# FFN gate/up products by Strassen's scheme: seven block products in place of eight, their mixed operands made on GpSimd, VectorE and ScalarE

## The reference, cut to what matters

```python
def rms_norm(x, g):
    y = xf * lax.rsqrt(jnp.mean(xf * xf, axis=-1, keepdims=True) + RMS_EPS)
    return (y * g.astype(jnp.float32)).astype(x.dtype)

def swiglu(u, wg, wu, wd):
    return (jax.nn.silu(u @ wg) * (u @ wu)) @ wd

for l in range(DEPTH):                      # DEPTH = 2
    hp = hp + 0.5 * swiglu(rms_norm(hp, norm_ffn1[l]), ffn1_wg[l], ffn1_wu[l], ffn1_wd[l])
    ...
    hp = hp + 0.5 * swiglu(rms_norm(hp, norm_ffn2[l]), ffn2_wg[l], ffn2_wu[l], ffn2_wd[l])
```

## Time and profile before

| what | value |
|---|---|
| median of 3 runs | 2280.02 us (2279.99 to 2283.45) |
| the profiled execution's span | 2286.5 us, 6.5 us over that median |
| TensorE busy | 2122.0 us, 93% of the span |
| VectorE, ScalarE, GpSimd busy | 57%, 28%, 10% |
| mean granted TensorE clock | 0.952 of 2.4 GHz |

### The profile page before, as it was taken

The page is one execution under the profiler, slowest core; times in us unless marked ns, Lnnn a source line. Parts: engine busy times, 40 slices in busy tenths (PEclk is TensorE's granted clock), DMA queues, the critical chain, the costliest instruction groups (busy, mean ns, idle before and its releaser), DMA issues.

```text
span 2286.5 us, 36127 instructions
## 1 busy us (share of the span) xinstructions
PE 2122.0 (93%) x14822; PEld 1614.0 (71%) x14822; DVE 1296.4 (57%) x1866; ACT 631.6 (28%) x630; POOL 230.5 (10%) x215
## 2 busy tenths in 40 slices
PE   6999989999997779899997999999899689999799
PEld 4777757665776746677775777777667467777577
DVE  7555566314987553555554646555655675555562
ACT  4222242112153241222224213222512032222410
POOL 1000020000047300000003000000110300000200
PEclk9999999997999789899998999999999789999899
DMA  3222212210221010022221212222222102222130
GB/s 146 92 84 82 104 58 96 82 47 10 65 65 42 15 74 19 28 83 92 92 93 63 102 55 74 89 76 92 87 85 73 53 21 92 92 91 87 70 108 37
DMA packets 23980, 166.46 MB, mean 73 GB/s; under 512 B 3024, under 2 KB 3024, under 8 KB 8176
## 3 DMA queue, kind: packets, MB, share of 16 engines
q1 hardware_dynamic: 22176, 157.98, 19.6%
q0 software_dynamic: 1744, 7.66, 1.0%
HBM read 161.80 MB, written 3.83 MB: 72 GB/s over the span
## 4 chain that ended last, share of the span: by engine, by line
PE 80%; DVE 9%; issue 5%; POOL 3%; ACT 2%; DMA 0%; ACTq 0%; DVEq 0%; SPq 0%; POOLq 0%
PE ps L1287 65%; PE ps L1281 6%; POOL arena L323 3%; DVE arena L1042 2%; DVE smalls L1041 2%; PE ps L1394 2%; PE ps L1473 1%; PE ps L1413 1%; PE ps L1589 1%; PE ps L1275 1%; PE ps L1549 0%; ACT wslot L485 0%; ACT arena L486 0%; DVE arena L1217 0%; PE ps L1377 0%
## 5 line engine op out<-in xcount | busy, mean ns | idle before, releaser
L1287 PE MATMUL ps<-normed,arena 128*128 128x296 f16 x8448 | 1073.0, 290 | 10.8 <-ACT normed L501 10.8
L1287 PEld LDWEIGHTS ps<-normed,arena 128*128 128x128 f16 x8448 | 830.1, 98 | 253.3 <-issue 11.5
L1287 PE MATMUL ps<-arena 128*128 128x296 f16 x4224 | 550.9, 295 | 50.4 <-POOL arena L323 45.5
L1287 PEld LDWEIGHTS ps<-arena 128*128 128x128 f16 x4224 | 418.4, 100 | 182.9 <-POOL arena L323 48.0
L486 ACT ACTIVATE arena<-wslot,scales 128x2048 f16<-128x2048 f32 (+1 forms) x112 | 238.7, 2131 | 366.2 <-PE ps L1287 238.9
L805 DVE TENSOR_REDUCE scales<-wslot 128x1 f32<-128x2048 f32 (+1 forms) x120 | 299.1, 2493 | 8.8 <-DMA wslot<-in_w_dn 8.7
L828 DVE SCALAR_TENSOR_TENSOR arena<-wslot,scales,arena 128x2048 f16<-128x2048 f32 (+1 forms) x112 | 282.0, 2518 | 33.2 <-ACT arena L486 32.1
L844 DVE SCALAR_TENSOR_TENSOR arena<-ps,scales,act_out 128x592 f32 (+1 forms) x88 | 73.3, 833 | 354.1 <-ACT act_out L494 353.8
L317 POOL PARTITION_ALL_REDUCE scales<-scales x120 | 49.7, 414 | 1597.2 <-DVE scales L805 1562.3
L1281 PE MATMUL ps<-normed,wslot 128*128 128x296 f32 x640 | 167.3, 423 | 1.5 <-DVE normed L773 1.0
L494 ACT ACTIVATE act_out<-ps,scales 128x592 f32<-128x592 f32 x88 | 66.2, 752 | 362.9 <-PE ps L1287 362.4
(11 more groups left out here) (250 smaller groups left out, 1301.7 us busy)
## 6 DMA issues: line engine op xcount, KB each, us to landing
wslot<-in_w_up SPq DMA_DIRECT2D x88, 1024.0 KB, 4.8
wslot<-in_w_dn SPq DMA_DIRECT2D x32, 1408.0 KB, 6.0
wslot<-in_w_in SPq DMA_DIRECT2D x20, 512.0 KB, 3.5
arena<-in_w_out SPq DMA_DIRECT2D x1, 4096.0 KB, 12.2
resid<-in_x SPq DMA_DIRECT2D x4, 592.0 KB, 6.6
out_y<-resid SPq DMA_DIRECT2D x8, 296.0 KB, 4.5
arena<-in_w_ai POOLq DMA_DIRECT2D x1, 2048.0 KB, 10.3
arena<-in_w_pool POOLq DMA_DIRECT2D x1, 1024.0 KB, 5.5
```

The lines of the kernel that those rows point to most:

```text
L1287: last = mm(ps[:, bank + hf, 0:HALF], w, x[:, hf * HALF:(hf + 1) * HALF], start=start, stop=stop)
```

## The change

The 22 gate/up units become 11 pairs, and a pair two steps: step `b` = 0 is the gate part of both units (256 output rows), step 1 the up part. A step's product is a 2x2 block product (two output row blocks, two halves of the 8 input chunks, two halves of the tokens). Eight block products would be 8 x 4 chunks x 3 parts = 96 matmuls; the Strassen form (Winograd's variant) takes seven, 84 matmuls, of mixed operands:

- the weight mixes `s1` to `s4` are made on GpSimd in `mix_weights`: four additions or subtractions of 512 float32 columns behind the `partition_all_reduce` of the same step. ScalarE splits the three plain blocks (`step_high1`, 1536 columns) and the four mixed ones (`step_high2`, 2048 columns), VectorE their low parts (`step_low1`, `step_low2`). Instead of the maximum on VectorE, ScalarE sums magnitudes (`step_bound`, 2048 columns).
- the activation mixes are made at the start of the FFN: 16 scalings of 296 columns, 6 mixes and 12 low parts of 592 columns on VectorE, 14 high parts on ScalarE (`x_highs`), and one mix and its low part on GpSimd (`mix_x`).
- the seven products are accumulated in three banks per step, with copies and sums between them (`keep_p1`, `keep_p5` on ScalarE; `sum_u2`, `sum_u3`, `sum_c22`, `sum_c12`, `sum_c21` on VectorE). The first pair has another order of the seven (`FIRST`), in which each operand is asked for as late as it can be.
- the hidden values are split while the last pairs run, `unit_low` is gone, and the down products need the second hidden scale only from chunk 12 on (`HEAD`).
- the buffers are laid out anew in one tensor `big`.

```diff
-            def unit_low(n, b):
-                pool.wait_ge(whigh_done, n + 1)
-                g.tensor_tensor(w16[:, b, 1, 0:DN_W], wslot[:, b, 0:DN_W], w16[:, b, 0, 0:DN_W], ALU.subtract)                     .then_inc(wlow_done, 1)
+            def mix_weights(n, step, b):
+                pool.wait_ge(step_max, step + 1)
+                g.partition_all_reduce(wall[:, b:b + 1], wmax[:, b:b + 1], P, ALL_MAX).then_inc(wall_done, 1)
+                a21, a11, a12, a22, s1, s2, s3, s4 = (wslot[:, b, i * QW:(i + 1) * QW] for i in range(8))
+                g.tensor_tensor(s1, a21, a22, ALU.add)
+                link(g.tensor_tensor(s3, a11, a21, ALU.subtract))
+                link(g.tensor_tensor(s2, s1, a11, ALU.subtract))
+                g.tensor_tensor(s4, a12, s2, ALU.subtract).then_inc(mix_done, 1)
...
             def ffn(f, ahead):
                 n0 = f * FFN_UNITS
-                for u in range(2, FC + 2):
-                    all_max(n0 + u, u % 2)
...
+                mix_x(f)
+                for u in range(2, FC):
+                    if u == 2 * HEAD_PAIRS + 2:
+                        hidden_max(f, 0)
+                    mix_weights(n0 + u, f * FC + u, u % 2)
+                for u in range(FC, FC + 2):
+                    all_max(f * DC + u - FC, u % 2)
+                hidden_max(f, 1)
...
+            def step_bound(stage, u, b):
+                a.activation(wslot[:, b, STEP_W:WSLOT], wslot[:, b, 0:STEP_W], ACT.Abs,
+                             accum_out=wmax[:, b:b + 1]).then_inc(step_max, 1)
...
+            def turn(stage, i, head=()):
+                step_high1(stage, 2 * i + 1, 1)
+                keep_p1(f, i, 0, FAST)
+                step_high2(stage, 2 * i + 1, 1)
+                keep_p5(f, i, 0, FAST)
+                if not last_turn:
+                    step_bound(stage, 2 * i + 2, 0)
+                silu_first(f, i, FAST)
...
             dve.wait_ge(s["out_sem"], 16 * 6)
-            first_unit(2)
-            update_residual(1, UNIT0[1] + IN_UNITS, 1.0)
+            first_units(2)
+            update_residual(1, DONE0[1] + IN_UNITS, 1.0)
...
+            def product_step(b, name, signal, first=False, x_waits=None):
+                q, x, at = PRODUCTS[name]
+                w = w16[:, b, :, q * QW:(q + 1) * QW].rearrange("p a (c n) -> p a c n", c=DC // 2)
+                out = ps[:, 3 * b + at, 0:HALF]
+                for c in range(DC // 2):
+                    mm(out, w[:, 0, c], xop[:, 0, x, c], start=start, stop=False, skip_group_check=True)
+                    mm(out, w[:, 1, c], xop[:, 0, x, c], start=False, stop=False, skip_group_check=True)
+                    last = mm(out, w[:, 0, c], xop[:, 1, x, c], start=False,
...
-                with pe.Fori(0, FC // 2) as i:
+                with pe.Fori(1, PAIRS) as i:
                     for b in range(2):
+                        for name in FAST:
+                            ready(i, b, name)
+                            product_step(b, name, prod_done[b])
```

More of the change, by code:

```diff
@@ new lines, in x_highs @@
+            def x_highs(f, q):
+                ready, each, first = X_READY[q]
+                for k in range(2):
+                    n = 2 * k + 2 if ready is x_scaled else k + 1
+                    act.wait_ge(ready, each * f + first + n)
+                    a.activation(xop[:, 0, q, 2 * k:2 * k + 2], X_FROM[q][:, 2 * k:2 * k + 2], ACT.Copy).then_inc(x_high, 1)
+            def turn(stage, i, head=()):
+                f = FFN_OF_STAGE[stage]
+                last_turn = isinstance(i, int) and i == PAIRS - 1
+                step_high1(stage, 2 * i + 1, 1)
[5 more added lines that the diff above has]
+                silu_first(f, i, FAST)
+                for c in head[:1]:
+                    act.wait_ge(hscale_done, 2 * f + 1)
+                    hidden_high(f, c, 0)
+                if last_turn:
+                    down_high(stage, FC, 0)
+                else:
+                    step_high1(stage, 2 * i + 2, 0)
+                keep_p1(f, i, 1, FAST)
+                silu_rest(f, i)
+                if not last_turn:
+                    step_high2(stage, 2 * i + 2, 0)
+                keep_p5(f, i, 1, FAST)
+                if not last_turn:
+                    step_bound(stage, 2 * i + 3, 1)
+                for c in head[1:]:
+                    hidden_high(f, c, 0)
@@ new lines, in first_units, with sum_u2 @@
+            def first_units(stage):
+                for b in range(2):
+                    weight_scale(stage, b, b)
+                    weight_back(stage, b, b, inv_x[:, stage:stage + 1])
+                    step_low1(stage, b, b)
+                    step_low2(stage, b, b)
+            def sum_u2(f, i, b, order):
+                dve.wait_ge(prod_done[b], 7 * i + 7 * PAIRS * f + order.index("P6") + 1)
+                dve.wait_ge(p1_done[b], i + PAIRS * f + 1)
+                if b == 0 and not (f == 0 and isinstance(i, int) and i == 0):
+                    dve.wait_ge(silu_done, i + PAIRS * f)
+                v.tensor_tensor(tmp[:, b, 0], ps[:, 3 * b + 1, 0:HALF], tmp[:, b, 1], ALU.add).then_inc(u2_done[b], 1)
```

628 lines of the change are left out of this document (425 added, 203 removed).

## The result

The changed kernel takes 2965.7 us (median of 4 runs, 2964.97 to 2966.98) against 2281.3 us for the kernel before on the same chip: a ratio of 1.3007, 95% interval 1.2988 to 1.3025. The forecast was 3064 us in a range of 2945 to 3230, so the sign and the mechanism held, and the forecast size was 98 us too high. The profiled execution has a span of 2963.8 us.

The account below looks back on a forecast made before the run. TensorE (93% busy) bound the kernel before; GpSimd's step would bound the changed one. 206.9 + 3 x 183.2 + 24.5 + 2.9 = +783.9 on 2286.5 gave 3070, less 6.5 for the median 3064 us; range 2945 to 3230.

Parts of the forecast that it names:

- the change of configuration in every step: GpSimd, each up step: switching from all-reduce to ordinary operation costs 7.15 us, the way back 8.88.
- One step of GpSimd, C: Each up step: change back, all-reduce, change forward and four mixes take 20.9 us, bounds 19.75 to 23.6.
- Nothing can hide it: GpSimd, every step: the 20.9 us are all its own sequence, twice TensorE's 10.7 us.
- M+4.8: In a step: next bound ready 4.8 us after the mixes of step u+1 end, all-reduce not before 8.9.
- The rival of cheap changes: GpSimd, all steps: configuration changes cost little, kernel faster at 2210 us (2170 to 2255); chance 0.06.
- Is another chain longer than C: Steps on ScalarE, VectorE, TensorE: none longer; TensorE at 1.2 GHz needs 20.7 us. Slower-chain rival: 3230 to 3470 us, 0.09.
- Head: Start of an FFN: activation scalings, mixes and low parts, `mix_x` ending about 23.5 us after the first scaling.
- S to M(2): FFN start: first activation scaling to the end of step 2's weight mixes, 23.5 + C = 44.4 us.
- Tail: End of an FFN: last weight mixes to the update that waits for the last down unit, 162 us.
- Stage 0: First FFN, nothing prepared ahead: step 2's mixes end 64.9 us after the first scaling; +206.9 us.
- Output projection: Stage 2: `first_units` holds VectorE until both steps are split, so TensorE waits for its first bank; +24.5 us.
- Stages 3 and 5: Norm there: VectorE waits for step 1's low part, +1.6 and +1.3 us.

Follow-up runs that it names:

- Experiment 1: Changed kernel with the all-reduce of a step's bound kept only in the first two of 22 steps of each FFN: 2347.3 us, 1.0285 of the kernel before.
- experiment 3: Kernel before with one GpSimd addition of four columns behind the all-reduce of each up step, no Strassen: 2440.5 us, ratio 1.0693.
- Experiment 4: Kernel before with the weight loads of the down units after the second narrowed to 256 columns: 2268.0 us in one run.
- experiment 5: Changed kernel with the up units' weight loads after the first two steps narrowed to 256 columns: 2921.7 us in one run.
- experiment 6: Changed kernel with each up step's bound and the first hidden bound summed on TensorE instead of all-reduced on GpSimd: 2286.8 us, 1.0025 of the kernel before.
- experiment 2: Changed kernel with the all-reduce of a step's bound in the even steps alone: 2650.1 us, 1.1621 of the kernel before.

## Why the prediction was right, and where its size was off

- *What bounds the kernel, and the change of configuration in every step*: right. Experiment 1 takes the changes away and 618 of the 684 us go with them; experiment 3 brings them into a kernel without Strassen and it becomes slower. The Trainium skill ("GPSIMD Engine Reference", section 2.1 Instruction dispatch) says that the first call to a freshly loaded kernel costs about 6 us, and the way back with little or no load beside it agrees (5.94 to 6.00); the way forward is dearer (6.98 to 7.85). That code is loaded at each change, as in the page's case, no run here shows. What I had made of that rule, 2735 us, would have been too low, since it took its price for both ways and 4.5 for the mixes.
- *One step of GpSimd, C = 8.88 + 0.38 + 7.15 + 4.5 = 20.9*: this is the term that was mis-sized. It measured 5.94 + 0.46 + 7.85 + 5.2 = 19.5. The way back is 2.94 below the rows it came from, the way forward 0.70 and the mixes 0.7 above. Experiment 4 shows why the rows misled: the 8.88 us held 3 us of a weight load. The DMA share of that turn in the earlier trace rows, 0.09, is a mean over 45 us, and I did not ask what ran in the 9 us of the change itself. The forward change had no load beside it in those rows, and in the new kernel it has one (experiment 5). The loops measured 370.9 to 372.4 us each against 397.5: 4 x 26 = 104 us too high, and that is nearly the whole miss (783.9 predicted, 677.3 measured between the two spans). The last step of the sum, 6.5 us off for the median, did not come true: the profiled execution of the changed kernel lies 1.9 us below the median, which brings 106.6 to 98.
- *The range, C from 19.75 to 22.7*: the measured 19.5 lies just below it, and start to start 19.6 in place of 20.9 is what the prediction itself had named as a sign of being wrong. The time stayed in the range because the range left 20 to 30 us for head and tail, and because a way back 2.9 us cheaper met a way forward and mixes together 1.4 dearer; that they nearly halved the error is luck.
- *Nothing can hide it*: too strong. The way back does lie beside the wait for the bound, 4.2 of its 6 us. I had listed the bound at M+4.8 and the all-reduce at M+8.9, so the overlap was in the sum, but not that taking the changes away would leave it standing. The rival of cheap changes, 2210 us, rested, among other things, on a VectorE that is never late; experiment 6, which is that kernel in effect, came to 2287.
- *Is another chain longer than C*: right that none is. TensorE's clock sank to 0.82 in the loop of stage 2, its matmuls to 154 ns, and it still waited 5.7 us in a step. The forecast of TensorE's busy time, near 1950 us or less, was wrong for this reason: it was 2195.6.
- *Head*: S to M(2) was put at 44.4 and was 43.65 in stage 2; `mix_x` ended at S+24.7 and not at 23.5 (the first activation mix on GpSimd took 7.4 us beside a busy VectorE, the second 1.4), C was smaller, and the two nearly balanced, which is luck as well. *Tail*: from the last mixes to the last update 162 predicted, 160.4 to 161.4 measured.
- *Stage 0*: M(2) at 24.7 + 64.9 = 89.6 predicted, at 90.08 measured. *Output projection*: 24.5 us were predicted (the marks in the text, 887.4 and 911.2, give 23.8). TensorE stood 21.08 us for the first bank (row below), and the whole stretch from the last update of stage 0 to the first scaling of stage 2 grew by 25.0 (527.4 us against 502.4 by the starts in the two traces). *Stages 3 and 5* began 4.6 us later each and not 1.6 and 1.3; why was not looked into.

TensorE's timeline in the output projection, after two of its eight units:

```profile
1089.17 3.33 PE L1581 MATMUL ps<-big 128*128 128x296 f32 x6 [21.08 <-DVE resid L996]
```

What stays open: how much of the 8.88 us a smaller or later load would have spared (one narrower width was tried in either kernel), what the chip does during a change, and whether Strassen's scheme can be made to pay. Experiment 6 leaves idle time in head and tail that another order of VectorE's work might fill; that wasn't tried.

## What to carry to other kernels

Before ordinary GpSimd work is added to a stage that calls an all-reduce, count how often the two alternate: each turn costs one change each way, some 14 us of GpSimd here, against 5 us for the work itself. Twenty turns a stage cost 155 us here (618 / 4), where the scheme saved 22 us of TensorE. A cost read from a trace carries whatever ran beside it; look at the DMA share of the very microseconds before it goes into a sum for a kernel where the load falls elsewhere. And a cost is worth on removal only what it exceeds the next wait behind it: take one away in every second step first, and the trace shows that next wait by itself.

## What the runs showed of the hardware

- A change of GpSimd between all-reduce and ordinary operation, by the means of the traces: 5.9 to 6.0 us back and 7.0 to 7.3 forward where the load was small or absent. With a load of 1.4 MB beside it the way back took 8.7 to 9.0 in the kernel before and 8.3 to 8.8 in experiment 3; with some 1 MB it took 6.25 there, and the way forward 7.9 in the changed kernel and 8.9 in experiment 2.
- It begins as soon as the operation before is done, also where the operation that it is for waits for another engine (1310.19 to 1316.26 with the bound ready at 1314.42; the 84 ways back in that trace before which the wait is named "issue" took 5.8 to 6.2 us).
- Additions of 512 columns on GpSimd took 1.26 us with VectorE idle and 1.8 in the mean with it busy (experiment 6, up to 3.0); VectorE's operation of 592 columns 0.83 us without and 1.84 with GpSimd's additions beside it, while its operation of 2048 columns stayed at 2.35.
- One column summed over the partitions by TensorE, two matmuls of together 0.28 us, served as the bound in place of an all-reduce of 0.38 us that cost 7.7 us a step with its changes (experiment 1).
